# HGRN2 scores in a four-layer transformer kernel: where the k-tiles of two gate projections stand between the score items

## What is computed

```python
rq, rk, rv, rg, gq, gf, gi, gg = _split_cols(h @ w_in, EV_SIZES)
...
lbb = lb.astype(jnp.float32)[None, :, None, :]
f = lbb + (1.0 - lbb) * jax.nn.sigmoid(f_logit.astype(jnp.float32))
log_f = jnp.log(jnp.maximum(f, F_FLOOR))
key = 1.0 - f
...
rel = cum[:, :, :, None, :] - cum[:, :, None, :, :]
w = jnp.exp(jnp.where(causal, rel, -jnp.inf))
scores = jnp.sum(qn[:, :, :, None, :] * kn[:, :, None, :, :] * w, axis=-1)
...
hg = _merge_heads(_head_rms_norm(hg, hg_norm_g)) * jax.nn.silu(gg.astype(jnp.float32))
```

## Time and profile before

| | us |
|---|---|
| median of three executions | 3126.01 |
| lowest, highest | 3124.66, 3126.16 |
| the profiled execution, whole | 3123.34 |
| its span from first to last instruction | 3121.6 |
| TensorE busy in the span | 3099.6 |
| VectorE busy | 1561.3 |
| ScalarE busy | 1064.0 |

### The profile page before, as it was taken

How to read it: one execution, slowest core, us unless ns; L and a number is a source line. 1 busy time by engine, 2 the same in 40 slices (tenths; PEclk the granted TensorE clock), 3 DMA queues, 4 the chain that set the end, 5 groups by cost and what they waited for, 6 DMA issues and landing times.

```text
span 3121.6 us, 37118 instructions
## 1 busy us (share of the span) xinstructions
PE 3099.6 (99%) x15548; PEld 2595.3 (83%) x15548; DVE 1561.3 (50%) x1887; ACT 1064.0 (34%) x1155; POOL 237.7 (8%) x139
## 2 busy tenths in 40 slices
PE   9999999999999999999999999999999999999999
PEld 7798988888889798888888778888888878888887
DVE  7564545554335654555435764544433766444432
ACT  3223344443222433444323332333323332333321
POOL 0002100010000020010000000111000000100100
PEclk9999999999999999999999999999999999999999
DMA  4411312222331141222233122222332322222222
GB/s 170 115 55 68 141 51 93 95 101 101 114 114 69 43 146 56 82 95 105 94 108 116 55 94 97 92 97 94 105 108 88 95 82 95 94 95 96 94 106 95
DMA packets 47567, 297.72 MB, mean 95 GB/s; under 512 B 7075, under 2 KB 7331, under 8 KB 13396
## 3 DMA queue, kind: packets, MB, share of 16 engines
q1 hardware_dynamic: 42336, 285.91, 25.9%
q10 hardware_dynamic: 5108, 10.02, 1.4%
HBM read 291.16 MB, written 4.75 MB: 95 GB/s over the span
## 4 chain that ended last, share of the span: by engine, by line
PE 91%; DVE 5%; ACT 2%; issue 1%; DMA 0%; POOL 0%; DVEq 0%; ACTq 0%; SPq 0%
PE G L460 83%; DVE wL L1701 1%; ACT wH L1268 1%; DVE mxt L1933 1%; PE psS L829 1%; PE psS L520 1%; PE psS L1030 1%; PE psS L1147 0%; PE G L1156 0%; PE G L1037 0%; PE psT L552 0%; DVE ws L2492 0%; PE psT L1183 0%; PE G L1071 0%; ACT ws L1359 0%
## 5 line engine op out<-in xcount | busy, mean ns | idle before, releaser
L460 PE MATMUL G<-hH,wH 128*128 128x512 f32 x2560 | 1016.9, 397 | 8.3 <-DVE wL L1701 3.3
L460 PE MATMUL G<-hH,wL 128*128 128x512 f32 x2560 | 999.7, 390 | 0.0
L460 PE MATMUL G<-hL,wH 128*128 128x512 f32 x2560 | 998.9, 390 | 0.0
L1701 DVE TENSOR_TENSOR wL<-raw,wH 128x2048 fp32r<-128x2048 f32 x260 | 626.5, 2410 | 635.9 <-ACT wH L1268 635.8
L460 PE MATMUL G<-wsr,wH 128*128 128x512 f32 (+1 forms) x2512 | 744.9, 380 | 1.3 <-DVE wsr L2321 0.9
L1268 ACT ACTIVATE wH<-raw 128x2048 fp32r<-128x2048 f32 x263 | 502.0, 1909 | 586.5 <-PE G L460 568.0
L460 PEld LDWEIGHTS G<-hH,wH 128*128 128x128 f32 x2560 | 482.1, 188 | 123.3 <-issue 21.2
L460 PEld LDWEIGHTS G<-hH,wL 128*128 128x128 f32 x2560 | 481.8, 188 | 102.5
L460 PEld LDWEIGHTS G<-hL,wH 128*128 128x128 f32 x2560 | 482.0, 188 | 99.5 <-issue 2.2
L460 PEld LDWEIGHTS G<-wsr,wH 128*128 128x128 f32 x2512 | 463.5, 188 | 92.0 <-DVE wsr L2321 1.8
L460 PE MATMUL G<-wsr,wL 128*128 128x512 f32 (+1 forms) x1256 | 475.8, 379 | 0.0
(11 more groups left out here) (291 smaller groups left out, 2511.2 us busy)
## 6 DMA issues: line engine op xcount, KB each, us to landing
raw<-in_units SPq DMA_DIRECT2D x263, 1024.0 KB, 4.8
ws<-bias_rows SPq DMA_DIRECT2D x2, 1536.0 KB, 14.6
bias_rows<-ws ACTq DMA_DIRECT2D x1, 2560.0 KB
x<-in_x SPq DMA_DIRECT2D x4, 512.0 KB, 7.9
ws<-in_mem ACTq DMA_DIRECT2D x2, 1024.0 KB, 4.8
ws<-bias_rows ACTq DMA_DIRECT2D x1, 2048.0 KB, 8.2
out_x<-x SPq DMA_DIRECT2D x3, 512.0 KB, 7.1
ws<-in_decay ACTq DMA_DIRECT2D x1, 1280.0 KB, 8.6
```

The source lines that it names most:

```text
L460: mm = pe.matmul(o, mv if swap else wt, wt if swap else mv, start=first and n == 0, stop=last and n == 2)
L1701: V.tensor_tensor(wL[:, g.p, :], raw[:, g.p, :], wH[:, g.p, :].bitcast(F32), ALU.subtract)\
```

## The change

TensorE's order alone is changed. The gate k-tiles leave their places behind the items h = 1 and h = 3; two k-tiles, 12 matmuls, stand behind h = 3 in each level. The items of a level then follow one another with nothing between them. The first gate job still begins in level 0 and ends behind level 3, the second begins in level 4 and ends behind level 7; within a level k runs in the same order as before. The other engines' streams are as they were.

```diff
@@ -829,15 +829,16 @@
                                 mm = pe.matmul(psS[:, n % 2, o:o + w], k_[:, ks:ks + P], q, start=True, stop=True)
                             mm.then_inc(hs_done, 1)
 
-                            if h % 2 == 1:
-                                k = n // 2 % KT
+                            if h == 3:
+                                k = lev % 4 * 2
                                 if k == 0:
                                     take_unit()
                                     take_job()
-                                for t in range(2):
-                                    w0 = k * 256 + t * P
-                                    mm = passes(G[:, c.job.p * 2 + t, :], w0, w0 + P, h_op, k, slice(0, S),
-                                                k == 0, k == KT - 1)
+                                for k in (k, k + 1):
+                                    for t in range(2):
+                                        w0 = k * 256 + t * P
+                                        mm = passes(G[:, c.job.p * 2 + t, :], w0, w0 + P, h_op, k, slice(0, S),
+                                                    k == 0, k == KT - 1)
                                 if k == KT - 1:
                                     end_job(mm)
                                     c.unit.off += 1
```

## The result

The changed kernel takes 3130.08 us, the one before 3124.76, each the median of 20 executions. The ratio is 1.0018, with a 95% interval of 1.0012 to 1.0024. So it is 5.3 us slower. That is clear of the noise, and its size lies just inside what the forecast called no change (6.25 us). The forecast was 3130.7 us and +4.65.

The account below looks back on a forecast made before the run. TensorE's stream, busy 99% of the span, was taken as the bound. Level terms 0.8 + 1.25 + 2.6 - 0.15 + 0.15 = +4.65 us on the median 3126.01 gave 3130.7 us, range 3127.6 to 3133.8.

Parts of the forecast that it names:

- the wait on the bank of the item two back: Third item of each level: due 1.71 us after the first, whose bank VectorE frees only at 2.15, so TensorE waits.
- Level 0: Third and fourth items wait while VectorE, still reading the value job, starts late; level ends at 206.95, not 206.15: +0.8 us.
- Level 1: VectorE makes a weight quarter behind each copy, so the fourth item waits longer; 7.60 us instead of 6.34, +1.25.
- Levels 2 to 5: Third and fourth items wait on VectorE; each level takes 7.00 us instead of 6.35, +0.65 each, +2.6 in four.
- Levels 6 and 7: Level 6, waiting on ScalarE, takes 4.80 us instead of 4.97, -0.15; level 7 takes 6.35 instead of 6.20, +0.15.
- Given back behind: Behind the levels, existing clock falls may land elsewhere, each worth 1.7 us either way; widens the forecast to +3.0 to +6.5.
- The restart behind a wait on VectorE: TensorE's delay from the releasing VectorE instruction's end to its next matmul: taken as 0.05 us, between 0.04 and 0.15.
- sizes in doubt: Restart and item lengthening over 11 waits on VectorE in levels 0 to 5: lower ends give +3.7 us, upper ends +6.0.
- the 0.08 of a saved switch: One TensorE switch from scores to gates goes in each level, worth 0.08 us; 0.2 in level 7.
- no wait at all: Rival: VectorE's bank reads always finish in time, so only switches go in the levels: 0.8 us saved, 3125.2 us; chance 0.06.
- The mark for VectorE's product on the first gate job: Sign expected in the profile after: this product starts at about 242.1 instead of 237.75.
- the clock falls: Rival: runs of 32 narrow matmuls with waits lower TensorE's clock in levels 1 to 5; two falls, +8.05 us, 3134.1; chance 0.10.

Follow-up runs that it names:

- the run with four banks: The changed order with the scores in four PSUM banks instead of two, against the changed kernel: 3123.55 us, ratio 0.9996 to the kernel before.
- eight items: Four banks, with 24 gate matmuls behind every second level so that eight items follow one another: 3124.16 us, ratio 0.9999 to the kernel before.

## Why the prediction was right

The forecast's step was the wait on the bank of the item two back, and its parts measured as follows, by the changed kernel's profile without a fall and its two others.

- **Level 0:** forecast +0.8, measured 7.20 against 6.35, +0.85.
- **Level 1:** forecast to be 7.60 long, measured 7.59. In two of the three profiles of the changed kernel a fall adds 1.6 and 3.1 us.
- **Levels 2 to 5:** forecast 7.00 each, measured 28.08 / 4 = 7.02; forecast +2.6, measured +2.7.
- **Levels 6 and 7:** forecast -0.15 and +0.15; level 6 takes 4.89 to 4.92 (-0.05), level 7 takes 6.35 or 6.36 (+0.15).
- **Sum:** forecast +4.65, by the trace without a fall +4.9, by executions of equal clock 4.7 to 5.8, by medians 5.3. The total came nearer (3130.7 against 3130.08) than the difference did by some luck: it was built on a median of three, 3126.01, where 20 executions gave 3124.76.
- **Given back behind:** no step gave anything back, as forecast. The stretch behind takes 2872.4, 2876.0 and 2874.9 us in the three profiles and 2872.6 in the one of before, where the clock differs, as the forecast had allowed for.

Two terms inside the levels were mis-sized, and nearly cancelled. The restart behind a wait on VectorE was put at 0.05 us from another stage. It took 0.14 to 0.15: 218.71 to 218.85 in level 2, and in level 0 from the end of the first bank's read (201.96 + 0.69 = 202.65) to

```profile
202.79 2.02 PE L829 MATMUL psS<-ws 128*128 128x128 f32 x16 [0.65 <-DVE ws L2250]
```

Against that the items behind a wait grew less than was said. The fourth item of level 2 waits too, briefly and as forecast. The timeline merges it with the third, but its records can be read apart:

```profile
219.29 0.42 DVE L2259 COPY_PREDICATED ws<-hmask,psS 128x256 f32<-128x256 int32 x1
...
219.65 0.28 PE L829 MATMUL psS<-ws 128*128 128x64 f32 x1
219.86 0.29 PE L829 MATMUL psS<-ws 128*128 128x64 f32 x1
```

Its bank is free at 219.71, it starts 0.15 later, and it takes 0.88 to the first gate at 220.74, where the forecast had 0.05 and 0.93. Only this last wait sets the level's end, so the forecast's sizes in doubt, which counted both waits of a level, were drawn about twice too wide. And the 0.08 of a saved switch does not exist: 0.02 a level by the run with four banks. In the sum for levels 2 to 5 it came in only once, through 2.86 for 12 gate matmuls, which was right. But the price of the rival **no wait at all** rested on it. Its kernel, the one with four banks, has levels 0 to 5 of 6.33, so 0.1 us saved there, not 0.5, plus level 6's own wait, 0.4.

The idle time was forecast at some 4.5 us in all. TensorE's waits of over 0.3 us in these levels are one of 0.65 and six of 0.39 to 0.53 (2.5 together): 3.2. The rest of the 4.9 is in shorter waits and longer items, so the mark was drawn too high though the levels' lengths agree. The mark for VectorE's product on the first gate job, a start at 242.1, does not follow from the forecast's own levels: 199.80 + 7.15 + 7.60 + 3 x 7.00 + 5.35 = 240.9, and 242.1 is its end. In the profile without a fall it starts 41.3 behind the first score, which is 241.1 on that scale.

The rival **the clock falls** had 0.10, was placed in levels 1 to 5, and was priced at 1.7 us a fall. It is there, in level 1 and in two of the three profiles of the changed kernel, at 1.6 us for one fall and 3.1 for one twice as long, so the mark "clock 1.00 throughout the levels" failed in these two and a chance of 0.10 was too low for it. As a share of the whole it stays small: the mean of the 30 executions is 3130.47 against 3124.55 of before, 5.9 more, of which some 5.0 stand at equal clock, so falls bring about 0.9. That the median is 5.3, only 0.4 over the waits' 4.9, though two of three profiles have a fall in level 1, is not accounted for: falls behind the levels differ by up to 3.5 us from one profile to the next, and no run separates them. Its condition was stated wrong. It took any level's narrow matmuls with waits for the condition, and priced two levels of five; the runs show no fall behind narrow matmuls alone (eight items) nor behind these with the short waits (levels 2 to 5), and falls behind those with the two waits of level 1. The Trainium skill (TensorE: Matmul & The Clock Gate, Why this matters for your kernels) lays drops in the middle of a kernel to long gaps between bursts. With the order changed in level 1 alone, the longest gap between 80 us and the fall was 0.53 us, so the measurement decides against that as the only cause. The same page (A second HAM failure mode: psum-queue depth-cycling) tells of small idle times between groups while the engine cycles through PSUM banks, which lower the clock too. By that rule levels 1 to 5 were places to suspect; the traces agree for level 1 and not for levels 2 to 5, whose wait of 0.39 us came with 1.00. The forecast did not weigh it.

The Trainium skill's remark on repeated gaps and too little PSUM (Perfetto Trace Analysis, Optimization Strategy) agrees with the traces: 0.39 us repeats in each of levels 1 to 5, and two more banks take all of it away. Copying first takes it away in levels 2 to 5 without any.

## What to carry to other kernels

When work that fills a gap is moved from between two users of a buffer ring to behind them, compare one distance with another: how long the consumer takes from an item's start to freeing its buffer (here 2.15 us), and when the producer will want that buffer again without the filler (1.71). The averages don't tell; VectorE was 71% busy before the change, and still late once the filler was gone. If the consumer is late, free the buffer earlier in its own order (copy first, then the work that needs no buffer) or take more buffers, before paying for a new order; but saved switches gave no time here that could be measured.

## What the runs showed of the hardware

A pair of switches between plain float32 matmuls of 64 columns and 512-column ones cost 0.02 us net (levels of 6.35 us with two pairs, 6.33 with one, none with a wait), though the first wide matmul behind the narrow ones takes 0.08 more than its neighbours. Narrow records start 0.11 us apart however long their run is; only the second follows the first after 0.05 to 0.06. TensorE restarts 0.14 to 0.15 us after the end of the VectorE instruction that it waited for, where in another stage 0.05 were seen. And the granted clock fell to half in level 1 or 3, in five of six profiles with two waits of 0.39 and 0.53 us in that level; in one of these TensorE had not paused for 125 us ahead of it.
